# A routed decoder step on one Trainium2 core: the fixed experts' first pick moved ahead of the ranking, and a lane's places spread nine apart

## What is computed

```python
scores = sigmoid(x @ router_w)                      # 576 x 64
biased = scores + router_bias
# best 4 of 8 groups by the sum of their two best, then the best 8 experts in those
gates = scores[chosen] / sum * 2.5
routed = sum over chosen experts e of gate_e * ((silu(x @ ex_w1[e]) * (x @ ex_w3[e])) @ ex_w2[e])
shared = (silu(x @ sh_w1) * (x @ sh_w3)) @ sh_w2
```

## Time and profile before

| what | value |
|---|---|
| median of 3 runs | 1017.95 us (1017.31 to 1018.47) |
| the profiled execution, its own time | 1016.82 us |
| its span | 1014.8 us |
| PE busy | 958.8 us (94% of the span) |
| DVE, POOL, ACT busy | 426.6, 344.0, 145.9 us |
| DMA | 297.50 MB, mean 293 GB/s |
| first and last loop matmul | from 339.4 to about 916 us |

### The profile page before, as it was taken

The page is one execution under the profiler, slowest core; times in us unless marked ns, Lnnn a source line. Parts: engine busy times, 40 slices in busy tenths (PEclk is TensorE's granted clock), DMA queues, the critical chain, the costliest instruction groups (busy, mean ns, idle before and its releaser), DMA issues.

```text
span 1014.8 us, 16186 instructions
## 1 busy us (share of the span) xinstructions
PE 958.8 (94%) x5994; PEld 418.5 (41%) x5994; DVE 426.6 (42%) x1215; ACT 145.9 (14%) x358; POOL 344.0 (34%) x439
## 2 busy tenths in 40 slices
PE   7999999999999799999999998989998899989996
PEld 5777655665554332233222333323232223333442
DVE  4311222345568533444334442333434244432885
ACT  4000023411021010100100000000100011102232
POOL 7000321310053544443444433344344344440132
PEclk9999999999999899999999999889999999999999
DMA  9033214222177989999999999999999999988932
GB/s 280 6 94 105 83 65 130 85 71 83 42 250 292 376 316 403 411 411 410 411 414 413 411 410 412 409 391 396 410 406 411 375 410 412 411 328 346 421 132 83
DMA packets 76115, 297.50 MB, mean 293 GB/s; under 512 B 15622, under 2 KB 26062, under 8 KB 49149
## 3 DMA queue, kind: packets, MB, share of 16 engines
q1 hardware_dynamic: 60133, 258.68, 65.3%
q0 software_dynamic: 15904, 37.79, 9.7%
HBM read 276.56 MB, written 31.50 MB: 304 GB/s over the span
## 4 chain that ended last, share of the span: by engine, by line
PE 63%; DMA 23%; DVE 5%; issue 4%; POOL 2%; SPq 1%; DVEq 1%; ACT 0%; POOLq 0%; ACTq 0%
PE bank L1978 22%; PE bank L2323 19%; DMA arena<-in_ex_w 9%; PE bank L2318 8%; DMA arena<-xs_dram,slot 6%; PE bank L2418 5%; DMA ring<-in_ex_w 5%; PE bank L1984 2%; POOL arena L994 2%; DMA arena<-y_dram 1%; DMA ring<-in_w_in 1%; PE bank L2161 1%; PE bank L2085 1%; PE bank L2075 1%; PE bank L2125 1%
## 5 line engine op out<-in xcount | busy, mean ns | idle before, releaser
L2323 PE MATMUL bank<-arena 128*32 128x512 f32 x1440 | 271.2, 609 | 9.7 <-DMA ring<-in_ex_w 4.3
L994 POOL DMA_INDIRECT arena<-xs_dram,slot x192 | 206.1, 1074 | 74.3 <-issue 62.0
L2323 PE MATMUL bank<-ring,arena 128*32 128x512 f32 x864 | 213.1, 609 | 4.4 <-DMA arena<-in_ex_w 4.4
L1010 POOL DMA_INDIRECT y_dram<-arena,outrow x46 | 47.1, 1023 | 269.2 <-DVE slot L1772 209.1
L2323 PE MATMUL bank<-xT,arena 128*32 128x512 f32 x576 | 114.3, 601 | 2.9 <-DMA ring<-in_ex_w 2.9
L2323 PEld LDWEIGHTS bank<-arena 128*32 128x32 f32 x1440 | 68.0, 112 | 111.3 <-issue 103.0
L1786 DVE STREAM_TRANSPOSE arena<-arena 128x1024 f32<-128x1024 f32 x48 | 59.7, 1244 | 88.3 <-DMA arena<-xs_dram,slot 88.3
L1978 PE MATMUL bank<-xT,ring 128*128 128x288 f32 x384 | 93.4, 406 | 0.7 <-DMA ring<-in_w_in 0.7
L2323 PE MATMUL bank<-mixpj,arena 128*32 128x512 f32 x384 | 84.7, 594 | 0.0
L1978 PEld LDWEIGHTS bank<-xT,ring 128*128 128x128 f32 x384 | 72.9, 190 | 20.9 <-DMA ring<-in_w_in 0.9
L2323 PEld LDWEIGHTS bank<-ring,arena 128*32 128x32 f32 x864 | 50.9, 112 | 49.7 <-issue 44.4
(11 more groups left out here) (417 smaller groups left out, 1237.0 us busy)
## 6 DMA issues: line engine op xcount, KB each, us to landing
arena<-in_ex_w SPq DMA_DIRECT2D x78, 1024.0 KB, 23.0
ring<-in_ex_w SPq DMA_DIRECT2D x50, 1024.0 KB, 20.1
xT<-in_ex_w SPq DMA_DIRECT2D x28, 1024.0 KB, 18.7
mixpj<-in_ex_w SPq DMA_DIRECT2D x24, 1024.0 KB, 20.1
arena<-y_dram SPq DMA_DIRECT2D x18, 1024.0 KB, 11.1
wide<-in_ex_w SPq DMA_DIRECT2D x12, 1024.0 KB, 25.2
ring<-in_w_in SPq DMA_DIRECT2D x5, 2048.0 KB, 8.1
ring<-in_w_out SPq DMA_DIRECT2D x2, 2048.0 KB, 8.5
```

The source lines that it names most:

```text
L994: pool.indirect_dma_start(xg[b][:, 256 * a:256 * a + 256], None, xs_quarter, bass.IndirectOffsetOnAxis(slot[k][:, a:a + 1], 0), bounds_che ...
L1010: pool.indirect_dma_start(y_dram, bass.IndirectOffsetOnAxis(outrow[b][:, 0:1], 0), og[b], None, bounds_check=K * T - 1, oob_is_err=False). ...
L2323: ins = pe.matmul(b[t, :], lhs[:, t], rhs(home(own if lane < 3 else common)), start=start, stop=stop)
```

## The change

Two edits in one.

**Places nine apart.** `iotaf` gets `25 * column & 31` in place of `column & 31`. Since 25 * 9 = 225 = 7 * 32 + 1, place n of a lane now sits in its partition 9n mod 32: a lane with few tokens has them spread over its 32 partitions. All that follows (slot, yrow, gate) is made per partition and follows of itself. The masking to 31 and the cast move from POOL to DVE, in the mixer stage.

**The fixed experts' first pick.** DVE first makes places, `tquo` and `tmod` for the three fixed experts alone, then the first one-hots, and ranks after that. POOL's split is cut in two, fixed experts first. The `tquo` and `tmod` of the other 61 experts are cast by ACT. PE makes the first pick three pieces into `first(2)`, the ranking's product after `first(2)`, and splits `first(3)` four and four around the second pick.

```diff
@@ psum_groups
-    g += [(("shT", 1), "s"), (("ord",), "v"), (("sh", 2), "s")]
+    g += [(("shT", 1), "s"), (("pk", 0), "v"), (("sh", 2), "s"), (("shT", 4), "s"), (("ord",), "v")]
     g += [(("pT", i), "s") for i in range(NT)]
-    g += [(("pk", 0), "v"), (("shT", 4), "s"), (("pk", 1), "v"), ...
+    g += [(("pk", 1), "v"), (("sh", 3), "s"), ...
@@ POOL
-            link(pool.iota(iotai.rearrange("p (q j) -> p q j", j=32), pattern=[[0, 4], [1, 32]], base=0,
-                           channel_multiplier=0))
+            link(pool.iota(iotai, pattern=[[25, P]], base=0, channel_multiplier=0))
-            pool.tensor_copy(iotaf[:, :], iotai)
...
-            split(1, 2, NT)
+            split(2, 2, NT, NE - FIXED, NE)
+            split(2, 2, NT, 0, NE - FIXED)
@@ ACT
             sh(3)
+            sht(NP_)
+            act.wait_ge(s_quo, 1)
+            act.copy(tquo[:, 0:NE - FIXED, :].rearrange("p e i -> p i e"), quo_i[:, :, 0:NE - FIXED])
+            act.copy(tmod[:, 0:NE - FIXED, :].rearrange("p e i -> p i e"), mod_i[:, :, 0:NE - FIXED]
+                     ).then_inc(s_table, 1)
+            act.wait_ge(s_table, 1)
             for i in range(NT):
                 b = full_bank(act, "pT", i)
...
-            sht(NP_)
             sh(4)
@@ DVE, in the mixer stage
+            link(dve.tensor_single_scalar(iotai, iotai, 31, ALU.bitwise_and))
+            dve.tensor_copy(iotaf[:, :], iotai)
@@ DVE, after weigh(late)
+            link(dve.scalar_tensor_tensor(out=t1_, in0=pos, scalar=1.0, in1=sel_, op0=ALU.add, op1=ALU.mult))
+            link(dve.tensor_scalar(place_i[:, :, fixed], t1_[:, :, fixed], -1.0, None, ALU.add))
+            table_of(fixed)
+            dve.wait_ge(s_split, 2)
             one_hots(0, 0, 0, heads[0], None)
+            dve.wait_ge(s_const, 5)
+            dve.scalar_tensor_tensor(out=keys, in0=count, ...).then_inc(s_keys, 1)
+            drain("v", dve.tensor_reduce(np_f[0:1, 0:1], ...), "pos")
             first_index(0)
+            dve.wait_ge(s_keys, 1)
+            ... the ranking, as before; places, quotients and remainders of the other 61 experts
+            b = full_bank(dve, "ord")
+            dve.tensor_scalar(order[0:1, 0:NE], b[0:1, 0:NE], 0.25, None, ALU.add).then_inc(s_order, 1)
             one_hots(0, 0, 1, heads[1], heads[2])
...
             first_index(1)
+            dve.wait_ge(s_table, 1)
+            dve.wait_ge(s_split, 3)
             one_hots(0, 0, 2, heads[3], None)
@@ PE
-            first(2, 0, 4)
-            ... ord
-            first(2, 4, KT)
+            first(2, 0, 3)
+            first_pick(0)
+            first(2, 3, KT)
+            turn_h(NP_)
+            ... ord, pT
-            first_pick(0)
-            turn_h(NP_)
-            first(3, 0, 3)
+            first(3, 0, 4)
             first_pick(1)
-            first(3, 3, KT)
+            first(3, 4, KT)
```

More of the change, by code:

```diff
@@ L415, in decoder_step @@
         s_ga, s_gb = sem("s_ga"), sem("s_gb")
+        s_keys, s_quo, s_table = sem("s_keys"), sem("s_quo"), sem("s_table")
         s_ring = [sem("s_ring0"), sem("s_ring1")]
@@ L921, in _, with split @@
             rms(3, NT)
[L923 to L928, removed]
+            def split(n, i0, i1, e0, e1):
+                pool.wait_ge(s_weigh, n)
+                gates = gt_[:, i0:i1, e0:e1]
+                parts = [tpick[:, e0:e1, i0:i1, c].rearrange("p e i -> p i e") for c in range(2, 6)]
+                pool.tensor_copy(parts[0], t2_[:, i0:i1, e0:e1])
                 for k in range(3):
@@ L934, in split @@
                 ins.then_inc(s_split, 1)
-            split(0, 0, 2)
+            split(1, 0, 2, 0, NE)
             rms(4, NT)
@@ new lines, in _ @@
+            dve.wait_ge(s_const, 5)
+            count = b[0:NE, NT * NE:(NT + 1) * NE]
+            dve.scalar_tensor_tensor(out=keys, in0=count, scalar=float(NE), in1=revs, op0=ALU.mult, op1=ALU.add
+                                     ).then_inc(s_keys, 1)
+            drain("v", dve.tensor_reduce(np_f[0:1, 0:1], b[0:1, NT * NE:(NT + 1) * NE], AX.X, ALU.max), "pos")
+            first_index(0)
+            dve.wait_ge(s_keys, 1)
+            link(dve.tensor_tensor(hits, keys, ident[0:NE, 0:NE], ALU.mult))
@@ new lines, in _ @@
+            link(dve.tensor_reduce(key_col, hits, AX.X, ALU.add))
+            link(dve.tensor_scalar(hits, keys, key_col, None, ALU.is_gt))
+            link(dve.tensor_reduce(rank_col, hits, AX.X, ALU.add))
+            dve.tensor_scalar(hits, rank_row, rank_col, None, ALU.is_equal).then_inc(s_order, 1)
+            link(dve.tensor_scalar(place_i[:, :, others], t1_[:, :, others], -1.0, None, ALU.add))
+            link(dve.tensor_single_scalar(quo_i[:, :, others], place_i[:, :, others], 5, ALU.arith_shift_right))
@@ L2286, in first_pick @@
                 pick(j + 1, j % 2, b, j, j > 0).then_inc(filled, 1)
+            positions()
+            turn_h(1)
+            first(2, 0, 3)
+            first_pick(0)
+            first(2, 3, KT)
+            turn_h(NP_)
+            pe.wait_ge(s_order, 1)
+            b = free_bank(pe, "ord")
+            pe.matmul(b[0:1, 0:NE], ids, hits, start=True, stop=True)
+            pe.matmul(b[0:1, NE:2 * NE], key_col, hits, start=True, stop=True).then_inc(filled, 1)
             pe.wait_ge(s_p, 16 * NT)
```

45 lines of the change are left out of this document (14 added, 31 removed).

## The result

The change made the kernel slower by a quarter of a per cent: 1021.13 us (median of 22 runs) against 1019.00 us (22 runs of the kernel before on the same chips), ratio 1.0023, 95% interval 1.0016 to 1.0031. The forecast was 1007.0 us.

A forecast was written before the change was run, and what follows sets the result against it. The prediction took the loop to be bound by saturated DMAs, their slowest engine delaying weight loads, with PE nearly as full. -8.8 us (loop) and -2.2 us (start) make -11.0, from 1017.95 to 1007.0 us; range 1002 to 1013.5.

The forecast's parts named there:

- The term of -8.8 us for the places nine apart: Loop: fullest DMA engine falls from 351 to 318 rows, saving 8.8 us between step 5 and step 36.
- the engine with the most rows is the slowest one: Loop: uneven gathered and scattered rows put the fullest DMA engine behind, and a weight load lands with its slowest share.
- 8.4 us worked out and 8.5 us measured at one load: Loop, step 17: fullest engine's surplus of 52.9 crossings, 8.4 us, against the slowest engine's lag in the trace, 8.5 us.
- the order that the prediction took: Gathers and scatters: block k of four partitions goes to DMA engine k mod 16; lanes 0 and 2 share eight engines.
- Rival 2: Loop: PE's own work ends last in half of the saved time; loop gains 4.4 us, 1011.4 us; chance 0.10.
- Rival 1: Loop: engines take blocks in another order, slowest engine stays; loop gains 0.6 us at most, 1015.5 us; chance 0.10.
- The term of -2.2 us for the early pick: Ahead of the loop: first gather 3.1 us sooner, loop starts at 337.2 us, 2.2 us sooner; bounds -3.1 and 0.
- I put the net at 0.1 (bounds 0 and 1.1): Ahead of the loop: PE's wait for the first one-hots, less short waits lost, delays the second pick by 0.1 us.
- rival 3: Ahead of the loop: DVE's ranking stalls beside POOL's split; loop starts 2.3 us late, 1020.2 us; chance 0.03.
- It costs nothing: Ahead of the loop: fifth home's load moves from 325 to about 327 us, needed over 40 us later; no cost.
- the measure of rows 4 and 5: Loop: slowest engine's lag, from bytes moved beyond a weight load when it lands; some 4 us forecast for 8.5.
- a loop within 2 us of the old 577 us: Loop: sign that the prediction is wrong, the loop's length staying within 2 us of 577.

The follow-up runs named there:

- The circle of turned orders: Kernel before, places still packed, every lane's places turned by one to seven blocks of four partitions: 1.0002 with one block, 1.0039 to 1.0068 with two to seven.
- The first pick alone: The changed kernel with the old `iotaf`, so without the places nine apart, against the kernel before: 1.0006 (0.9990 to 1.0022).
- one block turned: Kernel before, places still packed, every lane turned by one block of four partitions, so that its eighth block has the most rows: 1.0002 (0.9988 to 1.0016).
- the late load: Kernel before with SP's load of the fifth home's weights also waiting for the pass count, near 333 us in place of 325: 0.9983 (0.9970 to 0.9995).

## Why the prediction was wrong

**The term of -8.8 us for the places nine apart measured 0.3 us the other way** (1.0003, by its interval -0.9 to +1.4 us), and this is where the forecast failed. Its step was: the engine with the most rows is the slowest one. It rested on one agreement, 8.4 us worked out and 8.5 us measured at one load. The circle of turned orders refutes it: the same largest count gives anything from 1.000 to 1.007. The prediction did name the case in which the term is nothing, "if the fullest engine is the same as before", but its slowest bound, 1009.2 us, kept the whole 8.8. Three things were overlooked.

- The agreement was chance. The same measure at the 145th load gives 3.06 MB, again 8.4 us, while the forecast's own count has the lag grow to 18 us by step 36. That could have been read from the trace of before.
- Even the count was wrong in a premise. The prediction gave partition 32a + j the row of lane a, place j, in both transfers. That holds for the scatter. The gather (L994) is four DMAs, one per lane, and each fills all 128 partitions: the group of 32 chooses the quarter of the row (`slot` adds `quarter`). So in the gather engine k and engine k + 8 carry the same, and lanes don't part. Corrected, with the order that the prediction took, the fullest engine goes from 702 crossings to 615 of a mean of 576, which would make the gain over the whole loop 13.8 us; the prediction's own count, 702 to 636, makes it 10.5. The error isn't what hid the gain; it shows how little the agreement was worth.
- The reading that fits, and that no run shows: something else delays particular engines, and the lag is the sum of both. In the packed order of before the rows would then be few where that is, and levelling takes rows from the fullest engines and gives them to those that are behind anyway. What delays them stays open.

Rival 2, PE taking over, was not it: PE still stands for 20.2 us for weights, as before. Rival 1 put the loop's gain at 0.6 us at most and was nearer, but for a reason that the runs don't bear out: by its order, too, all turned kernels have the same largest count, and with the gather counted rightly its fullest engine would have been relieved as well (719 crossings to 662).

**The term of -2.2 us for the early pick measured +1.9 us at the loop's start.** With the 0.9 us by which all of this execution is later taken off, the gather was issued at 323.2 us, forecast 323.0, and the one-hots began at 317.4, forecast 317.2. Failed: "I put the net at 0.1 (bounds 0 and 1.1)" for PE's wait for them. It was 3.49 us. The one-hots took 3.5 us in place of 1.3, since they ran beside POOL's casts: the copy of L1714 took 1.69 us there and 0.17 later, L1719 1.29 and 0.82. That is rival 3's mechanism, put at 0.03, on other instructions than it named; its loop start, 2.3 us late, and its time without the gain of the lanes, 1020.2 us, came nearest to what was measured. And a wait that was priced as idle time alone cost PE's clock too: ten matmuls took 2.8 us longer. All this stands ahead of the ranking's product, and so of `order`, the second pick and the pass count. The second pick ended at 335.0 us, by the forecast at 329.1 + 0.9 = 330.0. That DVE would be the next in line was right; it was free at 339.0 us, by the forecast at 334.9, and those 4.1 us are the whole miss of this term.

**"It costs nothing"** of the late fifth home was near: alone, it gains 1.7 us, for a reason that the prediction only brushed ("the idle DMAs then serve the first gather alone"). The changed kernel couldn't use it, since DVE was free only at 339.0 us and began the transpose without a wait.

**Seen right:** the packets, the gather's start, that the measure of rows 4 and 5 would shrink at step 17 (by 2.0 us, where 4.5 were forecast), and what would prove the forecast wrong: a loop within 2 us of the old 577 us. It took 579 us.

The sum as it came: 1.9 us at the start, 0.3 in the lanes, 2.2 us beside 2.1 us between the medians. It leaves out the loop, which was 2 us longer in the profiled executions, and single executions differ by up to 5 us, so this agreement is again no proof. The first pick alone measured +0.6 us by its ratio (-1.0 to +2.2), the places nine apart +0.3 (-0.9 to +1.4).

## What to carry to other kernels

A count that agrees with one measured number is a guess. Work it out for a second point of the trace, where it would differ, before a term rests on it. To learn whether a load is uneven over engines that the profile doesn't tell apart, turn the data round the engines: the sums stay, and if the time moves, the largest sum isn't what sets it. And where a wait is added on TensorE, price the matmuls behind it at half clock as well, and fill the wait with work that is there.

## What the runs showed of the hardware

- **Where the rows stand matters to the DMAs here.** The same rows, turned by blocks of four partitions, cost 0.4 to 0.7% in six of seven positions. The Trainium skill, "DMA: Bandwidth & Descriptors", section "Latency and other measured facts", says that DMA engines 7 and 15 are usually slower in traces, and gives a guess at the cause. The runs fit with some being slower. That it is this pair alone doesn't fit: in the order that the prediction took both serve the eighth block of every lane, and with one block turned this block is the fullest, at 1.0002. The trace also has 48 packets of 16 KB on one instruction queue and 30 of 8 KB on another; on which engine they lie no row tells, and this was not tried.
- **DVE beside POOL.** A copy of 128 x 25 took 1.69 us beside POOL's casts of 183 columns, 0.17 us without them. The Trainium skill, "GPSIMD Engine Reference", section "2. Architecture", says that GpSimd and DVE share one read port and one write port of SBUF. The rows fit that, though no row shows a port.
- **TensorE's clock.** In the changed kernel PE was idle for 3.49 us up to 321.93 us, and its granted clock was 0.50 from 321.4 to 327.7 us. With no idle time at that place the clock stayed at 1.00 up to 325 us.
- **A first gather alone on the DMAs** had its rows there over 3 us sooner than beside 3 MB of weights: the transpose began 19.0 us behind the places with the late load, 22.3 before.
